# The recurrence's triangular inverse on two 64-row diagonal blocks, side by side in 64 columns

## The reference

```
def step(state, inp):                       # over 512 positions
    r_t, w_t, k_t, v_t, a_t, b_t = inp
    sa = einsum('bhij,bhj->bhi', state, a_t)
    state = state * w_t[:, :, None, :] + sa[..., None] * b_t[:, :, None, :] + v_t[..., None] * k_t[:, :, None, :]
    y = einsum('bhij,bhj->bhi', state, r_t)
    return state, y
```

## Time and profile before

| what | us |
|---|---|
| median of 3 runs | 2572.45 |
| lowest and highest of them | 2572.36, 2576.35 |
| the profiled execution's own time | 2578.01 |
| its span, first to last instruction | 2576.2 |
| PE busy | 2336.0 (91%) |
| PEld busy | 1190.4 (46%) |
| DVE busy | 883.2 (34%) |
| ACT busy | 503.6 (20%) |
| POOL busy | 384.5 (15%) |
| mean granted TensorE clock | 0.948 |

### The profile page before, as it was taken

How to read it: one execution, slowest core, us unless ns; L and a number is a source line. 1 busy time by engine, 2 the same in 40 slices (tenths; PEclk the granted TensorE clock), 3 DMA queues, 4 the chain that set the end, 5 groups by cost and what they waited for, 6 DMA issues and landing times. The chain is left out here.

```text
span 2576.2 us, 23241 instructions
## 1 busy us (share of the span) xinstructions
PE 2336.0 (91%) x8683; PEld 1190.4 (46%) x8683; DVE 883.2 (34%) x1484; ACT 503.6 (20%) x941; POOL 384.5 (15%) x746
## 2 busy tenths in 40 slices
PE   6998988999998979999769899889769999999985
PEld 3444654443443434443343788734434444444432
DVE  3547832222220220005888233442631111111116
ACT  2013642111110010003145222200111111111121
POOL 0004000400000000000000000000044444444424
PEclk9998999999999989997879999899889999999997
DMA  8502003354323011212101780120269999899867
GB/s 354 217 20 106 1 1 150 129 196 170 130 84 131 34 67 65 76 70 91 33 35 70 311 322 1 41 106 17 82 251 380 387 393 372 347 416 393 339 258 284
DMA packets 68545, 446.28 MB, mean 173 GB/s; under 512 B 12227, under 2 KB 12883, under 8 KB 43505
## 3 DMA queue, kind: packets, MB, share of 16 engines
q0 software_dynamic: 36176, 254.42, 25.0%
q1 hardware_dynamic: 32290, 190.78, 19.4%
HBM read 416.27 MB, written 73.45 MB: 190 GB/s over the span
## 5 line engine op out<-in xcount | busy, mean ns | idle before, releaser
L2455 PE MATMUL psum<-arena 128*64 128x512 f32 (+1 forms) x1088 | 360.2, 594 | 0.0
L938 PE MATMUL psum<-arena 128*128 128x512 f32 x704 | 307.1, 596 | 3.3 <-PEq L870 3.3
L2455 PEld LDWEIGHTS psum<-arena 128*64 128x64 f32 (+1 forms) x1088 | 138.7, 164 | 185.0 <-issue 184.8
L938 PEld LDWEIGHTS psum<-arena 128*128 128x128 f32 x704 | 133.2, 191 | 177.2 <-issue 177.2
L2446 PE MATMUL psum<-arena 128*64 128x512 f32 (+1 forms) x544 | 186.2, 598 | 1.2 <-ACT arena L2488 1.2
L1176 PE MATMUL psum<-arena 128*128 128x512 f32 x384 | 166.8, 597 | 3.6 <-ACTq L1221 3.6
L1068 PE MATMUL psum<-arena 128*128 128x512 f32 x352 | 153.5, 598 | 7.0 <-PEq L157 7.0
L997 DVE SCALAR_TENSOR_TENSOR arena<-psum,arena 128x511 f32<-128x511 f32 x88 | 66.0, 750 | 253.1 <-ACT arena L972 251.5
L1791 PE MATMUL psum<-arena 128*128 128x128 f32 x1024 | 128.1, 287 | 19.9 <-DVE arena L1879 19.9
L2516 DVE TENSOR_TENSOR arena<-arena,psum 128x256 f32<-128x256 f32 x51 | 21.5, 421 | 340.8 <-ACT arena L2484 340.8
L1791 PEld LDWEIGHTS psum<-arena 128*128 128x128 f32 x1024 | 124.1, 201 | 24.5 <-DVE arena L1879 21.5
(11 more groups left out here) (491 smaller groups left out, 2980.9 us busy)
## 6 DMA issues: line engine op xcount, KB each, us to landing
scratch_expert_out<-arena SPq DMA_DIRECT2D x18, 2048.0 KB, 23.5
scratch_expert_out<-arena SPq DMA_DIRECT2D x51, 512.0 KB, 9.6
arena<-in_w_ada SPq DMA_DIRECT2D x12, 2048.0 KB, 21.2
arena<-in_ada_w POOLq DMA_DIRECT2D x12, 2048.0 KB, 8.4
arena<-in_w_up SPq DMA_DIRECT2D x22, 1024.0 KB, 5.0
arena<-in_w_in SPq DMA_DIRECT2D x9, 2048.0 KB, 8.1
arena<-in_w_down SPq DMA_DIRECT2D x5, 2048.0 KB, 8.2
arena<-in_w_o SPq DMA_DIRECT2D x2, 2048.0 KB, 8.0
```

What stands on the lines that cost most here:

```text
L938: last = pe.matmul(K.bank[2 * (n % 3) + half], w[:, k, P * half:P * half + P], K.h[:, k, :], start=(k == 0), stop=(k == KD - 1))
L2455: last = pe.matmul(K.bank[2 + s][r, :], xt[:, s, P * k + r.start:P * k + r.stop], gu[:, lane, 2 * E_FF * k:2 * E_FF * (k + 1)], start=(k = ...
```

## The change

The triangle is now treated as two diagonal blocks of 64 rows and a corner block of 64x64, per head. The two diagonal blocks are inverted by the table of steps as before, but stacked in one tile: block 0 in rows 0 to 63, block 1 in rows 64 to 127, both in the same 64 columns. So a step has 16 products of 64x64 (8 heads, 2 blocks), block 0 in the array's first rows and columns, block 1 in its last rows and columns, and copies and adds of 256 columns a group where they had 512. The table has 14 steps: the off-diagonal part needs powers only to the 3rd. The corner block is joined at the end: transposes of the first block's inverse (line 1840 of the new kernel), the raw corner times the second block's inverse (1843), and the product of both (1856), copied into the upper right of `tt`. In the front, D and D' come from 32 products of 64x64 in all four quarters of the array; the first step waits for D and D' alone. The products for mh move into the steps (after steps 2 and 4), the raw corner's (`cross`) after step 7. Y is made in two halves, with the joining product between. GpSimd prepares four half masks and clears the lower left of `tt`. The copies are waited for one step sooner (i - 2 for i - 4), as the steps now rotate over 4 PSUM banks.

```diff
     steps = [
         ("D'", "D", "D2", False), ("D", "D'", "D2'", False), ("D2'", "D2", "D4", False), ("D2", "D2'", "D4'", False), ("D4", "D4'", "D8'", False),
-        ("D2'", "Q", "Q", True), ("D4'", "Q", "Q", True), ("D8'", "Q", "Q", True), ("Q", None, "D4'", False),
-        ("D4'", "F", "D", False), ("F", "D4'", "D'", False), ("D'", "D", "D2", False), ("D", "D'", "D2'", False), ("D2", "D2'", "D4", False),
-        ("D'", "Q", "Q", True), ("D2'", "Q", "Q", True), ("D4", "Q", "Q", True)]
+        ("D2'", "Q", "Q", True), ("D4'", "Q", "Q", True), ("D8'", "Q", "Q", True), ("Q", None, "Q'", False),
+        ("Q'", "F", "N", False), ("F", "Q'", "N'", False), ("N", "N'", "N2'", False),
+        ("N'", "Q", "Q", True), ("N2'", "Q", "Q", True)]
...
+    STEP_BANKS = (0, 1, 2, 5)
+    MIXED_AFTER, CROSS_AFTER = {2: 0, 4: 1}, 7
...
+            def small(h, q, bank, at, left, i, right, j):
+                rows, out = slice(64 * h, 64 * h + 64), slice(64 * i, 64 * i + 64)
+                return pe.matmul(K.bank[bank + h][out, at + 64 * q:at + 64 * q + 64], left[rows, q, 0, now.start + 64 * i:now.start + 64 * i + 64],
+                                 right[rows, q, 0, now.start + 64 * j:now.start + 64 * j + 64], start=True, stop=True)
...
-                products(c, 0, 0, 0)
+                for left, right, at in ((bk, ar, 0), (ar, bk, 256)):
+                    for q in range(4):
+                        for i in range(2):
+                            for h in range(2):
+                                last = small(h, q, D_BANK, at, left, i, right, i)
+                pr_mm.by(last)
...
-                pe.wait_ge(pr_out.sem, PRODUCTS * c + PRODUCTS)
+                pe.wait_ge(d_out.sem, 2 * c + 2)
                 for i, (left, right, _, _) in enumerate(steps):
                     for g in range(2):
-                        if i >= 4:
-                            after_step(pe, c, i - 4, g)
+                        if i >= 2:
+                            after_step(pe, c, i - 2, g)
...
                         for h in range(4):
-                            out, a = K.bank[(2 * i + g) % 8][:, C * h:C * h + C], inv[left][:, g, C * h:C * h + C]
-                            if right is None:
-                                last = pe.transpose(out, a, K.ident[:, :])
-                            else:
-                                last = pe.matmul(out, a, inv[right][:, g, C * h:C * h + C], start=True, stop=True)
+                            for rows in (slice(0, 64), slice(64, P)):
+                                at = slice(256 * g + 64 * h, 256 * g + 64 * h + 64)
+                                out, a = step_bank(i, g)[rows, 64 * h:64 * h + 64], inv[left][rows, at]
+                                if right is None:
+                                    last = pe.matmul(out, a, K.ident[rows, rows], start=True, stop=True)
+                                else:
+                                    last = pe.matmul(out, a, inv[right][rows, at], start=True, stop=True)
                         st_mm.by(last)
+                    if i in MIXED_AFTER:
...
+                        mixed(c, g)
+                    if i == CROSS_AFTER:
+                        pe.wait_ge(mh_out.sem, 2 * c + 1)
...
+                                last = small(h, q, CROSS_BANK, 0, ar, 1, bk, 0)
+                        cross_mm.by(last)
...
+                pe.wait_ge(t_out.sem, 4 * c + 4)
+                pe.wait_ge(cross_out.sem, c + 1)
                 for h in range(HEADS):
+                    last = pe.transpose(K.bank[FIRST_BANK][0:64, 64 * h:64 * h + 64], tt[0:64, h, 0:64], K.ident[0:64, 0:64])
+                first_mm.by(last)
+                for h in range(HEADS):
+                    last = pe.matmul(K.bank[CORNER_BANK][0:64, 64 * h:64 * h + 64], cross[64:P, 64 * h:64 * h + 64], tt[64:P, h, 64:P], start=True, stop=True)
+                corner_mm.by(last)
...
+                outputs(0)
+                pe.wait_ge(first_out.sem, c + 1)
+                pe.wait_ge(corner_out.sem, c + 1)
+                for h in range(HEADS):
+                    last = pe.matmul(K.bank[JOINED_BANK][0:64, 64 * h:64 * h + 64], first_turned[0:64, 64 * h:64 * h + 64], corner[0:64, 64 * h:64 * h + 64], start=True, stop=True)
+                joined_mm.by(last)
+                outputs(1)
+                pe.wait_ge(joined_out.sem, c + 1)
```

More of the change, by code:

```diff
@@ L1698, in phase_recur @@
     K.memory.release("small_r", "second_r")
-    inv = {name: low[:, 1024 * i:1024 * i + 1024].rearrange("p (g n) -> p g n", g=2) for i, name in enumerate(("D", "D'", "F", "D2", "D2'", "D4"))}
-    inv["D4'"] = row[:, 0:1024].rearrange("p (g n) -> p g n", g=2)
-    inv["D8'"] = row[:, 1024:2048].rearrange("p (g n) -> p g n", g=2)
+    names = ("D", "D'", "F", "D2", "D2'", "D4", "D4'", "D8'", "Q", "Q'", "N", "N'", "N2'")
+    inv = {name: low[:, 512 * i:512 * i + 512] for i, name in enumerate(names)}
+    first_turned, corner, cross = (row[:, 512 * i:512 * i + 512] for i in range(3))
     tt = row[:, 2048:3072].rearrange("p (h t) -> p h t", h=HEADS)
-    inv["Q"] = row[:, 2048:3072].rearrange("p (g n) -> p g n", g=2)
     gb = row[:, 3072:4096].rearrange("p (h t) -> p h t", h=HEADS)
@@ L1731, in after_step @@
         if steps[i][3]:
-            engine.wait_ge(st_dve.sem, 2 * (len(adds) * c + adds.index(i)) + g + 1)
+            engine.wait_ge(st_dve.sem, 2 * ((len(adds) - 1) * c + adds.index(i)) + g + 1)
         else:
@@ L1746, in _, with mixed @@
         def _(pe):
-            def products(c, u, j, g):
+            def mixed(c, g):
                 for q in range(2):
@@ L1762, in _ @@
                     tr_pe.by(last)
-                products(c, 0, 0, 0)
+                for left, right, at in ((bk, ar, 0), (ar, bk, 256)):
[4 more added lines that the diff above has]
+                pr_mm.by(last)
                 if c:
                     pe.wait_ge(y2_out.sem, c)
-                products(c, 1, 0, 1)
+                for q in range(4):
+                    for h in range(2):
+                        rows = slice(64 * h, 64 * h + 64)
+                        last = pe.matmul(K.bank[GB_BANK + h][:, C * q:C * q + C], bk[rows, q, 0, now], ar[rows, q, 1, now], start=True, stop=True)
+                gb_mm.by(last)
                 if c:
@@ L1855, in _ @@
             dve.wait_ge(gr_out.sem, gr_out.n)
-            spread_mask = lambda m, n: masks[:, m, :].unsqueeze(1).to_broadcast([P, n, P])
+            dve.wait_ge(masks_halved.sem, 8)
             for c in range(NCH):
[L1858 to L1872, removed]
-                for g in range(2):
-                    dve.wait_ge(pr_mm.sem, 5 * c + 4 + g)
-                    pr_out.by(dve.tensor_tensor(mh.rearrange("p (g q h) v t -> p g h q (v t)", g=2, q=2)[:, g], K.psum[:, 512 * UNIT_BANKS[2 + g]:512 * UNIT_BANKS[2 + g] + 1024].rearrange("p (h q n) -> p h q n", h=2, q=2),
@@ new lines, in halved @@
+                def halved(name, v, m):
+                    return dve.tensor_tensor(eight(inv[name]), two(D_BANK).rearrange("p (h v q t) -> p h v q t", h=2, v=2, q=4)[:, :, v],
+                                             half_masks[:, m, :].unsqueeze(1).unsqueeze(1).to_broadcast([P, 2, 4, 64]), ALU.mult)
+                dve.wait_ge(pr_mm.sem, c + 1)
+                d_out.by(halved("D", 0, HALF_D))
+                d_out.by(halved("D'", 1, HALF_DT))
+                f_out.by(halved("F", 0, HALF_F))
```

110 lines of the change are left out of this document (76 added, 34 removed).

## The result

| | before | after |
|---|---|---|
| median of 4 runs, us | 2574.4 | 2533.74 |
| lowest to highest | 2572.36 to 2577.74 | 2527.29 to 2545.82 |
| profiled execution, its span | 2578.01, 2576.2 | 2545.82, 2544.0 |
| mean granted clock | 0.948 | 0.939 |
| the four chunks, us | 57.91, 57.83, 57.82, 58.28 | 61.58, 56.88, 38.60, 38.79 |

The ratio after to before is 0.9839, interval 0.9819 to 0.9859: 40.7 us faster, where 8.3 were forecast. A chunk is counted from its first transpose to the next chunk's. The four together fell from 231.84 to 195.85 us, 36.0 less. The profiled execution is only 32.2 faster: the recurrence began 4.1 us later (1436.79 for 1432.65), as it does by a few us in either direction in every profile of this study, and what follows the chunks took 911.7 us before and 911.4 now.

A forecast was written before the change was run, and what follows sets the result against it. It took TensorE, busy 91% of the span, as the bound. A chunk of 55.6 us against 57.8 saves 2.2, four times 8.8, less 0.5 for POOL: 8.3, giving 2564 us; 8-in-10 range 2515 to 2600.

The forecast's parts named there:

- front: Each chunk's transposes, 64 small passes and two masks before the first step: about 4.7 us, before 11.1.
- one dependent step: A step needing the one just made, at high clock: 1.23 us, TensorE working 0.9 and waiting 0.33; before 1.79.
- 14 steps with mask blocks and cross: Inverse steps with two blocks of mask products, cross products and one 1.1 us wait: 18.9 us, against 34.3.
- tail: From X to the chunk's end: transposes, corner and joining products and tiling changes add 3.0 us, giving 15.4.
- high-clock chunk: One recurrence chunk if the clock stays high: 4.9 + 18.9 + 15.4 = 39.2 us.
- gain per chunk at high clock: Saving in each of four recurrence chunks before any loss by the clock: 18.6 us.
- Small pass: 64x64 passes in the steps: two in opposite corners go side by side, 0.056 us a pair; bounds 0.056 to 0.112.
- Rival C: Opposite corners, writing one bank, don't go side by side: 87 us a chunk, 118 more in all, 2690; chance 0.10.
- Hidden edits: Later masks (F, sum, gb, mh) run beneath the steps; uncovered they'd cost 3 to 4 us; one wait of 1.1 us.
- The clock takes most of it back: In each chunk thin work drops the clock between steps 3 and 7, low through U: 55.6 us against 57.8.
- Rival A: The clock holds through the chunks: four times 18.6, 74 us less, 2498; chance 0.12.
- Rival B: After U the clock does not come back, next front and steps start low: 67.6 us a chunk, 2611; chance 0.14.

## Why the prediction was wrong

The direction was right, and the terms that the timeline could give came out close. Chunk 3 of the profiled execution, at full clock, against the steps of the forecast:

| step of the forecast | forecast | measured |
|---|---|---|
| front | 4.9 | 4.07 (1555.25 to 1559.32) |
| one dependent step | 1.23 | 1.22 |
| 14 steps with mask blocks and cross | 18.9 | 18.98 (to 1578.30) |
| tail | 15.4 | 15.55 (to 1593.85) |
| high-clock chunk | 39.2 | 38.60 |
| gain per chunk at high clock | 18.6 | 19.2 |

*Small pass.* A pair in 0.056 was right (0.058), from a row with another tile. In the front four went abreast, so its 64 passes took 1.02 and not 1.4; that and shorter hand-overs are the 0.8 of the front, which the forecast gave as about 4.7, 4.9 and 4.6 in three places. The 18.9 of the steps is partly luck: its items, ten dependent steps at 1.23, four at 0.9, two mask blocks at 1.2, 0.45 and 1.1, make 19.9. A block took 1.07 (1562.53 to 1563.60), and the wait 0.78.

*Rival C*, the corners one after the other, was wrong: both corners write one bank and overlap. The Trainium skill's "TensorEngine Tiling (Array Packing)", "Gotcha 1: PSUM Pressure", says different row tiles can't use one bank at once. Here two row tiles did, in different partitions of it, and the measurement decides.

*Hidden edits.* The later masks lie beneath the steps; the wait for one of them, forecast at 1.1 a chunk, was 0.8, and taking it away gave 0.7 to 1.1 in three chunks of four. Making the first step wait for gb gave back 2.3 to 3.5.

*The step that failed: "The clock takes most of it back".* It put the fall between step 3 and step 7 in every chunk, out of thin work alone, and worked out 55.6 a chunk. The runs show in its place:

- thin work holds the clock. With the writes ahead, four chunks of it ran at 1.00 throughout, pauses of 0.8 us included. The reading of the earlier trace rows was too wide: L1971 and L1308 show work that didn't raise a clock which was already low. Nothing in them shows the clock falling under such work, and in the earlier trace rows X and U of the old kernel, the same thin shape, had held it.
- the steps even raise it. In chunk 1, and behind the pause put in by hand in chunk 4, it went from 0.50 to 1.00 under 64x64 products alone (1462.63 to 1465.63; 1586.45 to 1589.46).
- it falls at pauses. Within the chunks of all ten traces TensorE stood idle for over 1 us 33 times. 26 of these gaps (1.19 to 5.02 us) had a fall inside them or at most 2.6 us behind their end, and no fall came otherwise; the pauses put in by hand did it with no traffic. Seven gaps were not followed by one: one of 3.27 us in chunk 2 of the new kernel, two of the four of some 2.8 in the fronts of the kernel that waits for gb, and four of 1.30 to 1.68.
- the pauses in the steps come from the writes, which keep TensorE's instructions back (below). Their place moved with them (chunks 1 and 2, then 3 and 4), and they went away with them.
- in chunks 1 and 2 the loss was as large as I had it, by another way: 61.58 and 56.88, for 55.6.

So the gain is two chunks of 19.2 and 19.5, less 2.7 for the first two together (3.7 lost, 0.95 won): 36.0 us. The forecast had 2.2 four times. What I had right of the clock was its second half: low from X on, it stays low at least until the state products. X to U took 21.65 us in chunk 1 (1471.73 to 1493.38), for 22.1. (The 10.2 "at high" that stood beside it was a slip of addition; its items make 12.0, and 11.98 was measured.)

*Rival A*, the clock holds, was what chunks 3 and 4 did, and what all four do without the writes: 2506 for its 2498. The Trainium skill's "TensorE: Matmul & The Clock Gate", "HAM oscillation — how this bites in real kernels", cited there, says that long idle between bursts is what re-throttles. These traces agree as to the idle time: all 26 falls stand at a gap. Two of them stand at gaps of 1.19 and 1.32 us, though, which is not long. *Rival B* never happened: where the clock was low in X, it came back in the state products or just behind them (1496.35 and 1554.38 in the new kernel), before the next front.

What the prediction lacked was a mechanism in the profile of before that could have been asked after. The earlier trace rows show the DMA engines at 0.92 through the old steps. I took that traffic for harmless, since nothing in the chunks waits for those writes. TensorE's own instructions do, and the change makes it need 2.7 times as many per us (18.8 by 7.0).

*Why TensorE stood idle under the writes.* Its instructions were late. The evidence is in the traces of the four kernels that have the writes beside the new steps (the new kernel, the writes after chunk 2, the corners in another order, the writes one at a time):

- Their chunks have 19 gaps of over 1 us. Each ends 1.16 to 1.60 us after the end of a packet of the instruction queue.
- Count every record of TensorE's queue, semaphore waits with it: all 19 gaps stand at the same place modulo 256, the size of a packet. In the new kernel 256, 256, 768, 512 and 256 records lie between one gap and the next. The pauses that were put in by hand or wait for a mask don't stand there.
- While the writes ran, no two packets were less than 6.97 us apart. In the new kernel with the writes moved ahead they came down to 3.8 us apart, with no gap. The old kernel's were never less than 8.3 us apart in its chunks, so it asked for none faster than the writes let them through.

**What stays open.** Why a packet waits for the end of a write, when the writes are paced, isn't shown, nor whether reads at this rate would do the same. No run changed the number of instructions alone. Why seven gaps were not followed by a fall is open too. And the profiled execution's gaps needn't be those of the others: the new kernel's runs differ by up to 18.5 us, those without writes by 4.3. That the number and place of gaps, and of falls behind them, varies would explain it, but only one execution has a trace.

## What to carry to other kernels

When a change makes many short instructions out of few long ones, look at what the DMA engines do in that stretch, even if nothing there waits for a transfer; bulk writes that no one needs yet belong in another stage (here worth 27 us by the medians, 30 by the ratios, and nothing to the old kernel). A row with a low clock under busy work shows only that this work doesn't raise it; ask for a row in which the clock falls, and look at the pause before. A pause costs by its place: 3.7 us cost 4.9 ahead of steps that brought the clock back, and 15.7 ahead of X to U, which did not. And when an engine idles with its operands ready, count its instructions from one gap to the next: a constant multiple points at their loading.

## What the hardware showed that was not expected

- 64 weight loads of 64x64 in opposite corners, alternating, took 1.97 us, their products in one PSUM bank; 64 in four quarters 1.02. In runs of four in one corner, 64 took 2.90.
- Beside DMA writes of 396 to 407 GB/s (282 to 302 where they were paced) TensorE starved for 1.2 to 3.7 us at a time, with its operands ready, in a stretch that takes 18.8 matmuls per us when undisturbed; at 7.0 per us it did not.
- The gaps stand a multiple of 256 instructions apart, one packet of 16 KB, and with the writes paced 14 of 16 such packets came just as a write ended.
- 64x64 products in two corners raised the clock from 0.50 to 1.00 (56 matmuls in 3.00 us ahead of the rise); X to U did not (116 in 20.90, most of them full-array products with 64 columns moving, the corner's between them).
- Full-array products with 64 columns moving held the clock at whichever level they met: 1.00 in U at 0.112 us per pass, 0.50 at 0.213, in a stretch of 20.90 us with no pause that has the corner's products in it too.

```profile
1489.96 3.62 PE L1863 MATMUL psum<-arena 128*128 128x64 f32 x16
```

```profile
1588.49 1.95 PE L1863 MATMUL psum<-arena 128*128 128x64 f32 x16
```

The same 16 passes of the new kernel, in chunk 1 and in chunk 3.
